# The delta rule's preparation placed in the gate chunks, and its first normalisation behind the second pass's last level

## What is computed

```
u = rmsnorm(x) @ w_in                    # fox q,k,v,z,f | rwkv r,kr,vr,z_b,w_down,a_down | g_a | g_b
o_a = fox_attention(...) * silu(z_a)
r, kr, vr, z_b, w_down, a_down = split(token_shift(u_rwkv))
w = -softplus(-(w0 + tanh(w_down) @ w2)) - 0.5;   decay = exp(-exp(w))
a = sigmoid(a0 + a_down @ a2)
kk = kr * k_k;  kk = kk / max(|kk| per head, eps)
kr = kr * (1 + (a - 1) * k_a)
per token: S = S * decay + (S @ -kk) (kk*a)^T + v k^T;   y = S @ r        # 16 heads of 64
y = groupnorm(y) * ln_w + ln_b;  bonus = sum(r * k * r_k) * v
o_b = (y + bonus) * silu(z_b)
m = sigmoid(g_a) * (o_a @ w_proj_fox) + sigmoid(g_b) * (o_b @ w_proj_rwkv)
out = rmsnorm(x + m @ w_out)
```

## Time and profile before

| | |
|---|---|
| runs | 3123.22, 3121.57, 3117.95 us (median 3121.57) |
| the profiled execution | 3119.44 us |
| its span | 3117.5 us |
| TensorE busy | 2993.9 us (96%) |
| VectorE, ScalarE busy | 1848.9 us (59%), 1371.2 us (44%) |
| mean granted TensorE clock | 0.977 of full |

### The profile page before, as it was taken

One profiled execution on the slowest core, in us unless ns is written; L12 is line 12 of the kernel. 1 busy time (PEld: TensorE's weight loads), 2 busy tenths in 40 slices (PEclk: granted clock), 3 DMA queues, 4 the chain that ended last, 5 costly groups with the idle time before them and its releaser, 6 DMA issues.

```text
span 3117.5 us, 45946 instructions
## 1 busy us (share of the span) xinstructions
PE 2993.9 (96%) x17935; PEld 2484.0 (80%) x17935; DVE 1848.9 (59%) x2047; ACT 1371.2 (44%) x1876; POOL 344.8 (11%) x371
## 2 busy tenths in 40 slices
PE   8999999999999987999999999999999999986898
PEld 6888788788888877888888888887888888765786
DVE  5555567856665769455555555556445664467664
ACT  5555454343444454444444344445444444422244
POOL 2000011930001948000000000000000000000000
PEclk9999999999999987999999999999999999988999
DMA  7555476675757984566566665655666678701364
GB/s 242 173 171 165 153 223 200 218 224 168 223 186 240 244 255 120 170 193 211 186 193 189 190 188 189 190 185 168 179 198 192 189 213 255 215 23 46 121 211 155
DMA packets 302691, 580.98 MB, mean 186 GB/s; under 512 B 21512, under 2 KB 40200, under 8 KB 300832
## 3 DMA queue, kind: packets, MB, share of 16 engines
q1 hardware_dynamic: 285696, 522.85, 54.5%
q0 software_dynamic: 9264, 37.29, 4.2%
q10 hardware_dynamic: 7536, 18.06, 1.9%
HBM read 550.35 MB, written 21.50 MB: 183 GB/s over the span
## 4 chain that ended last, share of the span: by engine, by line
PE 90%; DVE 6%; ACT 1%; issue 1%; POOL 1%; DMA 1%; ACTq 0%; SPq 0%; DVEq 0%; POOLq 0%
PE acc L940 26%; PE acc L947 26%; PE acc L941 26%; PE tp L955 2%; DVE wL L2260 2%; PE acc L1568 1%; PE acc L1569 1%; PE acc L1575 1%; PE tp L1481 1%; PE acc L1479 1%; PE wk L1226 0%; POOL xs L883 0%; DVE A L3049 0%; PE acc L1241 0%; DMA raw<-in_a_w_in_dram 0%
## 5 line engine op out<-in xcount | busy, mean ns | idle before, releaser
L2260 DVE TENSOR_TENSOR wL<-raw,wH 128x1024 fp32r<-128x1024 f32 (+1 forms) x968 | 1227.4, 1276 | 1124.8 <-ACT wH L1603 1122.9
L1603 ACT CAST wH<-raw 128x1024 fp32r<-128x1024 f32 (+1 forms) x968 | 1009.6, 1045 | 1416.2 <-PE acc L947 1227.2
L940 PE MATMUL acc<-wH,xH 128*128 128x512 f32 (+1 forms) x2208 | 866.5, 393 | 7.0 <-DVE xL L2314 4.2
L941 PE MATMUL acc<-wH,xL 128*128 128x512 f32 (+1 forms) x2208 | 856.8, 389 | 0.0
L940 PE MATMUL acc<-wH,hH 128*128 128x512 f32 x1536 | 603.5, 393 | 1.9 <-DVE hL L2314 1.9
L941 PE MATMUL acc<-wH,hL 128*128 128x512 f32 x1536 | 600.0, 391 | 0.0
L947 PE MATMUL acc<-wL,xH 128*128 128x512 f32 (+1 forms) x2208 | 588.1, 388 | 1.2 <-DVE wL L2260 1.2
L940 PEld LDWEIGHTS acc<-wH,xH 128*128 128x128 f32 x2208 | 415.9, 188 | 94.9 <-issue 5.0
L947 PEld LDWEIGHTS acc<-wL,xH 128*128 128x128 f32 x2208 | 413.1, 188 | 87.5 <-DVE wL L2260 1.9
L941 PEld LDWEIGHTS acc<-wH,xL 128*128 128x128 f32 x2208 | 416.1, 188 | 82.8
L947 PE MATMUL acc<-wL,hH 128*128 128x512 f32 x1536 | 412.4, 390 | 5.8 <-DVE wL L2260 5.7
(11 more groups left out here) (461 smaller groups left out, 2195.3 us busy)
## 6 DMA issues: line engine op xcount, KB each, us to landing
raw<-in_mlp_w_dram SPq DMA_DIRECT2D x512, 512.0 KB, 3.8
raw<-in_w_in_dram SPq DMA_DIRECT2D x192, 512.0 KB, 3.8
raw<-in_a_w_in_dram SPq DMA_DIRECT2D x96, 512.0 KB, 3.8
raw<-in_b_w_glu_dram SPq DMA_DIRECT2D x64, 512.0 KB, 3.6
raw<-in_a_w_out_dram SPq DMA_DIRECT2D x32, 512.0 KB, 3.7
raw<-in_w_out_dram SPq DMA_DIRECT2D x32, 512.0 KB, 4.5
raw<-in_w_proj_fox_dram SPq DMA_DIRECT2D x16, 512.0 KB, 4.8
raw<-in_w_proj_rwkv_dram SPq DMA_DIRECT2D x16, 512.0 KB, 4.4
```

The costliest lines, as they stand in the source:

```text
L940: nc.tensor.matmul(bank, aH[:, k, rows], wH[:, j % SPLIT, u, 0:n], start=k == 0, stop=False)
L941: nc.tensor.matmul(bank, aL[:, k, rows], wH[:, j % SPLIT, u, 0:n], start=False, stop=False)
L1603: nc.scalar.copy(wH[:, j % SPLIT, :, 0:n], raw[:, j % RAW, :, 0:n]).then_inc(high_done, 1)
L2260: nc.vector.tensor_tensor(wL[:, j % SPLIT, :, 0:n], raw[:, j % RAW, :, 0:n], wH[:, j % SPLIT, :, 0:n].bitcast(F32), ALU.subtract).then_inc ...
```

## The change

- `steps` in the gate chunks gives way to `slot_chunks` (the renamed `fox_chunks`) on ScalarE and VectorE and to `between=` on TensorE. `prep_slot(p)` runs the preparation of pass m at s = (p - 3) % 10, so pass 0 in slots 3 to 12 and pass 1 in slots 13 to 22. TensorE: s 0 lin, 2 cum, 4 tot, 6 and 8 the transposes. ScalarE: s 1 sqrt, sigmoids, cast; 3 the exps; 5 lam; 7 and 9 the copies. VectorE: s 0 to 6.
- Tiles are made anew in place of shared, one set per pass, in other areas. One tile `par` takes k_k, k_a and r_k in turn; POOL's queue loads them (`delta_parameters`), each behind a wait for the step that read the one before.
- The bias rows become row 97 of `lin` (`lT` gets a row of ones, `lw2` a row of biases), and L3016 goes. The sigmoids read PSUM.
- `cum` is two matrices in place of three, strictly above and below the diagonal, by float32r in two terms (`sgH`, `sgL`: a ScalarE cast and a VectorE subtract per pass), 8 matmuls for 6; E1 and E2 come from the first sum plus `sg` (VectorE `sum`).
- The sigmoid of z_b and its product (`sz`, `zz`) move to slots 5 and 10.
- In the delta rule: the turns of `fo` are interleaved with the scores of pass 0; the scores of pass 1 wait for `S` and, from the third group on, `Y` and `O` of pass 0; `Y` stands ahead of `S`; `end(0)` stands behind pass 1's last level and before its `R`; the gate reads are issued ahead of `end(1)`.

```diff
-            fox_chunks(slot, second_out)
+            slot_chunks(slot, lambda k: second_out(9 + k))
...
-            steps(8, gate_out_of)
+            slot_chunks(prep_slot, lambda k: second_out(17 + k))
...
+            def prep_cum(m):
+                wait(name_dve=("sgL", m))
+                wait(("siga", m))
+                for e in range(2):
+                    for q in range(2):
+                        nc.tensor.matmul(bank, decayR[:, e], sgH[m][:, cols], start=True, stop=False)
+                        last = nc.tensor.matmul(bank, decayR[:, e], sgL[m][:, cols], start=False, stop=True)
+            def prep_tot(m):
+                wait(("E3", m))
...
+                if s == 1:
+                    act.wait_ge(r_dve, RDVE["kks", m])
+                    RACT.mark(r_act, nc.scalar.activation(rsm[:, 1], rsm[:, 0], ACT.Sqrt), "sqrt", m)
+                    act.wait_ge(r_pe, RPE["lin", m])
...
+                if s == 3:
+                    act.wait_ge(r_dve, RDVE["sum", m, 1])
...
+                    act.wait_ge(r_dve, RDVE["bon", m])
+                    factor("E0", bt[m], 0, m)
+                    factor("E3", par, 2, m)
...
+            def delta_parameters():
...
+                for m in range(MT):
+                    if m:
+                        pool.wait_ge(r_dve, RDVE["kt", m - 1])
+                        bcast("rwkv_k_k_2", par[:], r_par_in)
+                    pool.wait_ge(r_dve, RDVE["kk0", m])
+                    bcast("rwkv_k_a_2", par[:], r_par_in)
+                    pool.wait_ge(r_dve, RDVE["ka", m])
+                    pool.dma_start(par[:], I["rwkv_r_k_2"].rearrange("o h n -> o (h n)").broadcast_to([P, H1])).then_inc(r_par_in, 16)
+                pool.wait_ge(r_pe, RPE["L", 0])
+                bcast("rwkv_ln_w_2", lnw[:], r_ln_in)
+                bcast("rwkv_ln_b_2", lnb[:], r_ln_in)
...
+                if m:
+                    end_mean(0)
+                    end_centre(0)
+                    end_square(0)
+                    end_sums(0)
+                    end_gated(0)
                 dve.wait_ge(r_pe, RPE["R", m])
```

More of the change, by code:

```diff
@@ L159, in rwkv_steps @@
 def rwkv_steps():
[L161 to L167, removed]
-    for m in range(MT):
[L170 to L177, removed]
+    pe, act, dve = [], [], [("one",)]
+    for m in range(MT):
+        pe += [("lin", m), ("cum", m), ("tot", m)] + [("T", m, i) for i in range(8)]
+        act += [("decay",)] * (m == 0) + [("sqrt", m), ("sigw", m), ("sgH", m), ("siga", m)]
+        act += [("sz", i) for i in range(MT)] * (m == 0)
+        act += [("E2", m), ("E1", m), ("E0", m), ("E3", m), ("lam", m)] + [("T", m, i) for i in range(8)]
+        dve += [("kk0", m), ("kk2", m), ("kks", m), ("kkm", m), ("kkr", m), ("kk", m), ("sgL", m)]
+        dve += [("ka", m), ("k'", m), ("b", m), ("sum", m, 0), ("sum", m, 1), ("bo0", m), ("bo1", m), ("bon", m)]
         dve += [("kkh", m), ("rh", m), ("bh", m), ("kh", m), ("bt", m), ("kt", m)]
-        pe += [("T", m, i) for i in range(8)]
-        act += [("T", m, i) for i in range(8)]
+        dve += [("zz", i) for i in range(MT)] * (m == 0)
+    ends = [[("mu", m), ("nm", m), ("yc", m), ("y2", m), ("vs", m), ("sr", m), ("yn", m), ("yw", m), ("yb", m),
+             ("bv", m), ("yv", m), ("ob", m)] for m in range(MT)]
+    for m in range(MT):
         pe += [("A", m, j) for j in range(4)] + [("L", m), ("AV", m)]
@@ L195, in rwkv_steps @@
         dve += [("O", m, e) for e in range(2)]
-    end(MT - 1)
+    act += [("sd", 1)]
+    dve += ends[1]
     return pe, act, dve
@@ new lines, in prep_tot, with prep_turn @@
+            def prep_tot(m):
+                wait(("E3", m))
+                for p in range(R_PAIRS):
+                    last = nc.tensor.matmul(C[0][:, 2 * p:2 * p + 2], sg[m][:, p * P:p * P + P], tot[:], start=True, stop=True)
+                RPE.mark(r_pe, last, "tot", m)
+            def prep_turn(m, part):
+                wait(("T", m, 3) if part else ("lam", m))
+                pairs = ((kkh[m][:], "kkh"), (rr[:, m], "rh")) if part else ((E1[m][:], "bh"), (E2[m][:], "kh"))
+                for i, (src, name) in enumerate(pairs):
+                    wait(name_dve=(name, m))
+                    for q in range(2):
+                        for p in range(4):
+                            c = 4 * q + p
+                            last = nc.tensor.transpose(C[2 * i + q][:, p * P:p * P + P], src[:, c * P:c * P + P], ident[:])
+                        RPE.mark(r_pe, last, "T", m, 4 * part + 2 * i + q)
@@ L1398, in _ @@
+            turn_half(fo, range(2))
             pe.wait_ge(acc_free, 2 * t.fill + 4)
[L1399 to L1405, removed]
             half = [slice(0, TC), slice(TC, P)]
@@ L2221, in _ @@
             load_gates(0)
+            end(MT - 1)
+            high_half(8)
             g0 = t.group
@@ L3010, in _ @@
                 step(TT(hd(kk[:]), hd(kk[:]), wide(rsm[:, 2]), ALU.mult), "kk", m)
-                dve.wait_ge(r_pe, RPE["lin", m])
-                dve.wait_ge(r_in, 32 * (m + 1))
-                for name, dst, par, b0 in (("linw", sg, w0p, 0), ("lina", sa, a0p, 2)):
-                    for q in range(2):
-                        cols = slice(q * NW, (q + 1) * NW)
-                        step(TT(dst[:, cols], B[b0 + q], par[:, cols], ALU.add), name, m, q)
-                if m:
-                    end(m - 1)
+                dve.wait_ge(r_act, RACT["sgH", m])
```

532 lines of the change are left out of this document (303 added, 229 removed).

## The result

The changed kernel took 3080.25, 3078.30, 3078.49 and 3082.22 us, a median of 3079.4. The kernel before has a median of 3120.19 over four runs, one of them taken beside the new ones. The ratio is 0.987, with a 95% interval of 0.9853 to 0.9887: faster, near the 3082 that was stated and inside 3068 to 3098. The profiled execution took 3080.25, where the sum had 3080.3. Its span is 3078.5 us against 3117.5, so 39.0 us went, where the sum had 39.1. A sum that meets its value this closely can do so by errors that cancel.

What follows compares the result with a forecast made beforehand. TensorE bounds the kernel, except in two serial preparations where VectorE and ScalarE set the time. Saved 74.7, less 22.4 work, 7.8 waits and 5.4 clock, gives 39.1 us saved: 3082 us, range 3068 to 3098.

Steps and rivals of the forecast that it cites:

- The serial part: After the gate chunks: preparation leaves, saving 33.2 us in pass 0 and 41.3 in pass 1; serial sum 74.7 saved.
- TensorE's work in the gate chunks: Gate chunks: moved lin, cum, tot and transposes cost 10.4 us a pass; 22.4 in all with ten slot entries.
- The waits: Gate chunks: TensorE stalls 2.1 us at cum and 1.3 at tot of pass 0, 4.4 at tot of pass 1; 7.8.
- The clock: Low clock costs 3.4 us in the gate chunks and 2.0 at the serial part's start; 5.4, bounds 0 and 12.
- The normalisation: Pass 0's, moved before pass 1's R update: yy 1.6 us late, final normalisation 1.2 shorter, 0.3 left.
- the gate reads: Serial part's end: reads issued ahead of the final normalisation, no longer before the next casts; 0.5 us back.
- Late parameters: Gate chunks: r_k and k_a taking 11.6 us delay VectorE, then TensorE at tot; 2 to 6 us a pass, 3090; chance 0.15.
- The drain at a table switch: ScalarE: each table switch takes 2.66 us, delaying cum and tot in slots 4, 6, 16; 5.1 us, 3087; chance 0.04.
- The rival that the clock stays low through the gate chunks: Stalls and small matmuls keep the gate chunks' clock at 0.50; slower, 3132 for 110 us, 3177 throughout; chance 0.03.
- The rival that nothing stalls: Gate chunks: slots drift apart by themselves, no stalls or clock loss; 52.3 us saved, 3069; chance 0.12.

Runs made afterwards that it cites:

- The first run: Changed kernel with the decay totals one slot later on TensorE (s 5 in place of s 4): median 3071.42 us, ratio to before 0.9856.
- the ninth: Changed kernel with decay totals one slot later, Sigmoids and cast sgH ahead of the Sqrt, sgL ahead of the key norms' reciprocal: median 3067.53 us, ratio to before 0.9835.
- the seventh run: Changed kernel with both passes' preparation one slot later, totals at s 5, last copies in the slot of their transposes: 3075.78 us.
- the eighth: Changed kernel with both passes' preparation one slot later, totals at s 5, and ScalarE's sd behind W's copies: median 3069.55 us, ratio to before 0.9849.

## Why the prediction was right, point by point

**The serial part.** Pass 0 was to save 33.2 and saved 33.0, pass 1 41.3 and 41.4. L3174 comes 11.1 us after the last gate product (forecast 10 to 11).

**TensorE's work in the gate chunks** was 22.4 in the sum and 21.4 measured (195.52 with no wait and no low clock, less 174.08). In that run the units with small work in them are longer than 2.72 us by 3.46 for lin, 1.82 for cum, 1.83 for tot and 1.79 for each half of the transposes: 10.7 a pass, where the sum had 10.4. The 1.5 us for ten entries into a slot are not there: behind the small work a product runs on at its pace.

**The waits** were to be 2.1, 1.3 and 4.4, and were 2.03, 1.24 and 3.97: 7.2 against 7.8. The first run removes the last two by their distance, the ninth the first by its queue. The 7.1 us of lead held; the seventh run shows where it ends.

**The clock** was mis-sized the other way. In the gate chunks 3.4 us were to be lost. The stretch has 34.2 - 21.4 - 7.2 = 5.6 left for it, with 10.2 us at low clock, half of which is 5.1. Here misled: behind that idle one piece of 3.4 us came, and behind the wait of 3.97, whose window above has TensorE busy 1.23 of 5.20 us, came 6.9. In all the gate chunks came out 0.6 us worse than forecast: work 1.0 better, waits 0.6 better, clock 2.2 worse.

In the serial part 2.0 were to be lost; there are 6.8 us at low clock in pass 0 and 3.4 in pass 1. Over the runs with the changed kernel's pass 0, L3174 to yy took 51.0, 51.8 and 51.9 us with none, 52.1 to 53.1 (five runs) with 3.4, 53.6 with 6.8. In pass 0 the piece among the levels cost 1.5 of the 2.8 us (33.48 against 31.92 in the levels). The other 1.2 are behind the levels, the second piece and Y's new place together. That place has no term in the sum, and by the run with Y back it costs 0.8 to 1.7 in this pass. In pass 1 the piece cost 0.2 (21.29 behind the levels against 21.05 without it; 21.36 and 21.72 in the ninth and the first run, which have one in the same place).

**The normalisation.** The forecast was 1.6 us at yy and 1.2 back at the end, 0.3 in all, and 0.5 for the gate reads. ScalarE's deviation started 5.2 us into it (forecast 5.3), L3202 has no idle ahead of it, and yy came 2.2 later: 2.0 for the normalisation and 0.2 of clock. The end is 1.0 shorter in place of 1.7; why 0.7 are missing was not tried, and 20.3 us at low clock lie in that stretch against 18.5 before, which is the size of it.

**Where luck comes in.** The gate chunks were 0.6 us worse than forecast, the serial stretches and the end 2.2 worse together (0.2, 0.8, 0.6 and 0.7, less 0.1), and the stretch ahead of the gate chunks, for which there is no term, 2.8 better. So the sum agrees to 0.1 us by chance, and to 3 us by its mechanism.

**The rivals.** Late parameters fell: k_k, k_a and r_k landed in 5.3 us each, somewhat under the 5.8 that I had as the lower bound. The DMA issues of r_k in the gate stretch (queue, count, KB each, us to landing):

```profile
par<-in_rwkv_r_k_dram POOLq DMA_DIRECT2D x2, 512.0 KB, 5.3
```

No engine waited for their arrival. The drain at a table switch fell too. In the changed kernel, ScalarE in slot 4:

```profile
2585.38 1.28 ACT L2201 ACT_TABLE_LOAD   x1
2586.67 0.21 ACT L2201 ACTIVATE rsm<-rsm 128x16 f32<-128x16 f32 x1
2586.91 1.28 ACT L2205 ACT_TABLE_LOAD   x1
2588.20 0.60 ACT L2205 ACTIVATE sg<-tp 128x512 f32<-128x512 f32 x1
```

Two switches took 2588.20 - 2585.38 = 2.82 us with the Sqrt. By the rule of the Trainium skill (ScalarE: Activation LUTs, "What ACT_TABLE_LOAD costs") they would, as an estimate from its drain of about 1.38 us, have taken some 2.7 us more, and the wait on sgL would have been near 4.8 in place of 2.03. The trace does not agree with that rule. The rival that the clock stays low through the gate chunks fell with 10.2 us of 208.3. The rival that nothing stalls gave the lower end of the range, and the ninth run reaches it: 3067.5 with every stall in the gate chunks taken out.

## What to carry to other kernels

Where an engine is full, small work laid among its products costs its own busy time and no more, as long as the other engines' answers take fewer units than lie between question and use; count those units in the order written out, for each pass by itself, because the slots of two passes fall differently on the chunk's borders. Before moving a step to a later slot, add up what the queue of the casting engine then holds without a cast in it. Behind a chain in which TensorE sets the time, 13 us of VectorE work cost 2.0 here, and 11.4 more in all when they stood open ahead of it. And before two stretches are compared, set their edges by the same unit of work, and look where in them the low clock lies: the first is worth 3 us here, the second 1.5.

## What the runs showed of the hardware that I had not expected

The same 3.4 us at low clock cost 1.5 us among the levels of the inverse, 0.2 to 0.7 behind them in pass 1, where VectorE's normalisation runs, and some 1.7 to 1.9 among products (the first run's gate stretch has 25.35 us more than before, of which 21.4 are work and 2.0 the wait).

The same wait is not always followed by a lower clock. TensorE's wait on sgL was 2.03 us in the changed kernel, with the matmuls behind it 0.23 apart, at full clock. In the first experiment it was 2.02, and the matmuls behind it are 0.43 apart:

```profile
2592.89 0.64 PE L1434 MATMUL tp<-sgH,decayR 128*128 128x512 f32 x1 [2.02 <-DVE sgL L3035]
2593.32 0.63 PE L1435 MATMUL tp<-sgL,decayR 128*128 128x512 f32 x1
```

The wait of 2.65 in the seventh run had no low clock behind it, the same one of 2.64 in the eighth had 3.4 us. Waits of 1.24 and 3.97 us had 3.4 and 6.8 in the changed kernel. So what a wait costs in clock was not the same each time here, and single executions of one kernel differ by some microseconds by it. The Trainium skill (TensorE: Matmul & The Clock Gate, "HAM oscillation — how this bites in real kernels") tells of a kernel whose clock falls back at every one of its waits. The traces here agree with it for the wait of 3.97 us and for some of the shorter ones, but not for all.
